# Two joined pairs of chunks instead of one in each feed-forward, with one plain chunk between them

## The chip, the cores and the metric

One Trainium2 chip; the kernel runs on one of its cores. The metric is the device time of one launch in microseconds, the median of three runs: 2022.09 us before (2021.98 to 2022.65). Five engines matter here, each with its own in-order queue: TensorE (PE, with its weight loads as PEld), VectorE (DVE), ScalarE (ACT) and SyncE (SP), whose queue starts the DMA transfers; GpSimd (POOL) has next to nothing to do.

## The reference

Two blocks are run one after the other on an input of 256 rows by 1024 columns in float32, each with two layers. A layer of the first block is a feed-forward, a hybrid mixer and a second feed-forward; a layer of the second block is a mixer, a cross attention and a feed-forward. That makes six feed-forwards: four in the first block (layer 0, layer 0, layer 1, layer 1) and two in the second. Both blocks have the same hidden width.

```python
def swiglu_ffn(h, w_gate, w_up, w_down):
    return (jax.nn.silu(h @ w_gate) * (h @ w_up)) @ w_down     # h: 256 x 1024, hidden width 2816

x = x + 0.5 * rms_norm(swiglu_ffn(rms_norm(x, g_pre), w_gate, w_up, w_down), g_post)
```

Only the feed-forwards are touched by the change.

## The kernel before

**Products in three passes.** Every float32 operand is split into a high part (rounded, made by ACT) and a low part (the rest, made by DVE as operand minus high part), and a product is high x high + high x low + low x high. So a weight tile of 128 x 2048 (1 MB, called a unit) costs one ACT instruction (`high`, L1421), one DVE instruction (`weight_low`, L2113) and 24 matmuls of 128x128 by 128x512: 4 blocks of rows by 3 passes by 2 halves of the 256 rows.

**Chunks.** The hidden width of 2816 is worked off in 11 chunks (0 to 10) of 256 columns. A plain chunk c has two units for gate and up, `("gu", c, 0)` and `("gu", c, 1)`, and one for the down projection, `("down", c)`. Between them ACT makes the silu (L1517), DVE the hidden product (`hidden`, L2198), then DVE takes it apart into 16-bit planes (`part`, L2209), SP's queue transposes the planes by DMA (`turn_halves`, L567 and L571), DVE puts them together again (`join`, L2223), and ACT (`hidden_high`, L1533) and DVE (`hidden_low`, L2204) split the result. The down unit of a chunk waits for that last step (`gT_ready`). It stands after gate and up of the next chunk.

**A joined pair.** For the chunk numbers in `PAIRS`, chunk c and chunk c+1 are made together. Gate of both chunks is one 1024 x 512 matrix and up another; with the 256 rows of the input cut in two, the 2 x 2 by 2 x 2 product of blocks is made with seven block products instead of eight, by Strassen's scheme in Winograd's form. A block product is half a unit: 12 matmuls (L876), and it has one `high` and one `weight_low` of its own. TensorE's order in a pair is 1, 5, 2, 6, then the down unit of chunk c-1, then 3, 7, 4. What the seven products need beside their operands:

- sums of the input's blocks, once per feed-forward: `rows_whole` (one DVE instruction of 128x2048, L2235), `row_sums` (four of 128x512, L2239 to L2242), their high part on ACT (`sum_hi`, L1563) and their low part on DVE (`row_sums_low`, two of 128x1024, L2246 and L2248);
- sums of the weights' blocks, four DVE instructions of 128x2048 for each pair: T1 (L2260), T2 (L2265), T4 (L2272), T3 (L2276). T1 needs the weights of products 1 and 7, T2 those of product 3 too, T4 those of product 2. Products 5, 6, 7 and 4 use T1, T2, T3 and T4;
- sums of the results: four DVE additions (L2280), one more (L2314), and the hidden products of the pair (L2309, and L2320 twice).

**Order and buffers.** The order of all engines is written out by hand. DVE's order in a pair (the function `pair` of the DVE part) is T2, T4, low 2, low 6, join(c-1), low of down c-1, hidden_low(c-1), T3, low 3 and so on; T1, low 1, low 5 and `hidden` and `part` of chunk c-1 stand in front of it, in the chunk before the pair. That chunk is made by `chunk`, or by `chunk_behind` where it comes right after another pair; a `chunk_behind` has the two joins of the pair in it. TensorE waits in a pair for `hid_ready` (hidden of chunk c-1) before product 1, for `low_ready` before each product and for `gT_ready` before the down unit. The raw weights have a ring of five slots, loaded by SP in the order of `ffn` and `pair` there, each when the unit that held its slot is done (`FREED_BY`); the high parts have a ring of four.

In the program before, `PAIRS = (5,)`: chunks 5 and 6 are a pair, all others are plain. The row sums are spread over chunks 2, 3 and 4. In the first feed-forward the ACT queue also starts the loads of constants and gains after chunk 2, and DVE makes the tables for rotary angles after chunk `HOOK`; in the third, ACT starts the load of the memory input ahead of chunk 2 (`memory_load`); in the fourth, DVE splits the turned memory (L2709) ahead of the first `hidden_low`.

Of the kernel before, what the change touches and what calls it, by code (L numbers as in the profile page):

```python
# [31 lines left out]
ACT = mybir.ActivationFunctionType  # L32
# [25 lines left out]
NEG = -1e30  # L58


PAIRS = (5,)
JOIN_ON_ACT = False
HOOK = 7


def _ffn_order():
# [139 lines left out]
def _program(ctx, nc, d, out, counted):  # L206
# [7 lines left out]
    done, after = S.done, S.after  # L214
# [301 lines left out]
    def _(sp):  # L516
# [45 lines left out]
        def turn_halves(L, n, c):  # L562

            sp.wait_ge(halves_ready, L.turns(n, c))
            if c in SECOND:
                for t in range(TT):
                    sp.dma_start_transpose(second_halves_T[:, t, :, :],  # L567
                                           second_halves[:, t, :, :].rearrange("p b n -> p (b n)")).then_inc(second_turned, 16)
                return
            for t in range(TT):  # L570
                sp.dma_start_transpose(halves_T[:, t, :, :], halves[:, t, :, :].rearrange("p b n -> p (b n)")).then_inc(  # L571
                    halves_turned, 16)

        def ffn(L, n, k0, wg, wu, wd, ffn_ahead=None):
            for kh in range(2):
                gate_up(L, k0 + kh, kh, wg, wu, 0)
            if ffn_ahead:
                turn_halves(*ffn_ahead, NCHUNK - 1)

            def chunk(c):  # L580
                if c - 3 in PAIRS:
                    turn_halves(L, n, c - 3)
                gate_up(L, k0 + AT["gu", c, 0], 0, wg, wu, c)
                if c - 3 in PAIRS:
                    turn_halves(L, n, c - 2)
                if c > 2 and c - 2 not in PAIRS and c - 3 not in PAIRS:
                    turn_halves(L, n, c - 2)
                gate_up(L, k0 + AT["gu", c, 1], 1, wg, wu, c)
                if c == 2:
                    turn_halves(L, n, 0)  # L590
                if c - 2 in PAIRS:
                    down(L, k0 + AT["down", c - 2], wd, c - 2)
                if c < NCHUNK - 2:
                    down(L, k0 + AT["down", c - 1], wd, c - 1)

            def pair(c):
                if c - 3 in PAIRS:
                    turn_halves(L, n, c - 3)
                    turn_halves(L, n, c - 2)
                square(L, k0 + AT["p", c, 1], wg, 0, c * FC)  # L600
                if c - 3 not in PAIRS:
                    turn_halves(L, n, c - 2)
                square(L, k0 + AT["p", c, 7], wu, 0, c * FC)
                square(L, k0 + AT["p", c, 3], wu, 512, c * FC)
                square(L, k0 + AT["p", c, 2], wg, 512, c * FC)
                turn_halves(L, n, c - 1)
                down(L, k0 + AT["down", c - 1], wd, c - 1)

            for c in range(1, NCHUNK - 1):
                if c in PAIRS:  # L610
                    pair(c)
                elif c not in SECOND:
                    chunk(c)
            end, c = k0 + U_FFN - 1, NCHUNK - 1
            for kh in range(2):
                gate_up(L, end - 4 + kh, kh, wg, wu, c)
            turn_halves(L, n, c - 2)
            for i in range(3):
                down(L, end - 2 + i, wd, c - 2 + i)
            turn_halves(L, n, c - 1)  # L620
# [789 lines left out]
    def _(act):  # L1410
# [100 lines left out]
        def ffn(L, n, j, k0):  # L1511
            f = L.ffn(n)
# [106 lines left out]
                hidden(0)  # L1619
            silu(L, k0 + 3, 1)  # L1620
            high(L, k0 + 4 + AHEAD)
            for c in range(2, NCHUNK - 1):
                if c in SECOND:
                    continue
                if c in PAIRS:
                    pair(k0 + AT["p", c, 1], c)
                    continue
                if memory_here(L, n) and c == 2:
                    memory_load()
                (chunk_behind if c - 2 in PAIRS else chunk)(k0 + AT["gu", c, 0], c)  # L1630
                if L.sub0 + j == 0 and c == 2:
                    gain(post_g, 0, 1, post_loaded)
                    at, width = CONST["inv_freq"]
                    for at, end in ((P, at), (at + width, CONST_ARRAY.shape[1])):
                        act.dma_start(const[:, at:end], d["const"][:, at:end]).then_inc(const_loaded, 16)
                if L.sub0 + j == 0 and c == 8:
                    rope()
                if memory_here(L, n) and c == (9 if NCHUNK - 3 in SECOND or NCHUNK - 4 in SECOND else 8):
                    memory_std(L.l)
# [454 lines left out]
    def _(dve):  # L2094
# [97 lines left out]
        def ffn(L, n, j, k0):  # L2192
# [41 lines left out]
            def rows_whole():  # L2234
                then(V.tensor_tensor(sums, flat(hT_hi[:, :, :]), flat(hT_lo[:, :, :]), ALU.add), "whole")  # L2235
# [136 lines left out]
            else:  # L2372
                weight_low(L, k0 + 2 + AHEAD)
                join(0)
                hidden_low(0)
            weight_low(L, k0 + 3 + AHEAD)
            hidden(1)
            part(1)
            weight_low(L, k0 + 4 + AHEAD)
            for c in range(2, NCHUNK - 1):  # L2380
                if c in SECOND:
# [794 lines left out]
```

## Time and profile before

| | us |
|---|---|
| median of three runs (lowest, highest) | 2022.09 (2021.98, 2022.65) |
| the profiled execution, whole time | 2023.4 |
| the profiled execution, span of the trace | 2021.6 |
| PE busy in the span | 2000.0 (99%) |
| DVE busy | 1589.3 (79%) |
| ACT busy | 1169.2 (58%) |
| granted TensorE clock, mean | 0.999 of full speed |

The six feed-forwards lie at about 12 to 191, 431 to 611, 611 to 791, 1029 to 1212, 1432 to 1612 and 1835 to 2015 us. The profile gives for each engine when it was busy and, for idle time, which engine or transfer ended it. A matmul of 512 columns is shown with some 0.39 us, but the matmuls overlap: their starts are 0.227 us apart, and counts and durations of a run of them tell the rate. The large DVE instructions are shown with 2.28 us and start 2.20 us apart.

### The profile page before, as it was taken

What the parts mean: (1) busy time and instruction counts of PE and PEld (TensorE: products, weight loads), DVE (VectorE), ACT (ScalarE), POOL (GpSimd) and SP (SyncE); (2) the same over time, 40 slices, a digit from 0 to 9 for tenths busy, and PEclk for the clock granted to TensorE, in tenths of its full rate; (3) what the DMA queues carried; (4) which work ended last, traced back from release to release, by engine and by line L of the source; (5) the groups of instructions that cost most, each with busy time, mean ns of one, the idle gap of its engine ahead of it and who ended that gap; (6) DMA issues with size and microseconds to landing.
All of it is one profiled execution on the core that took longest, in us unless ns stands there. A gap on an engine that the chain in (4) does not pass through costs nothing.

```text
span 2021.6 us, 24239 instructions
## 1 busy us (share of the span) xinstructions
PE 2000.0 (99%) x9442; PEld 1639.1 (81%) x9442; DVE 1589.3 (79%) x2024; ACT 1169.2 (58%) x1438; POOL 0.2 (0%) x4
## 2 busy tenths in 40 slices
PE   8999999999999999999999999999999999999998
PEld 6788887888888888887888888888888887888887
DVE  6896899778867877899768967966788679667885
ACT  6455657664546555666564646756645466566453
POOL 0000000000000000000000000000000000000000
PEclk9999999999999999999999999999999999999999
DMA  8766764567777675764557767554667674546764
GB/s 261 235 204 183 225 201 146 171 194 208 221 211 240 202 229 171 225 189 146 186 184 208 223 184 212 189 157 148 191 214 215 190 226 161 176 141 186 223 211 121
DMA packets 339122, 394.54 MB, mean 195 GB/s; under 512 B 123824, under 2 KB 235072, under 8 KB 339008
## 3 DMA queue, kind: packets, MB, share of 16 engines
q1 hardware_dynamic: 334912, 381.94, 61.8%
q10 hardware_dynamic: 4096, 11.05, 1.5%
q8 instruction: 75, 1.23, 0.3%
q14 instruction: 39, 0.32, 0.1%
HBM read 365.66 MB, written 1.05 MB: 181 GB/s over the span
## 4 chain that ended last, share of the span: by engine, by line
PE 88%; DVE 6%; DMA 2%; ACT 2%; issue 1%; SPq 1%; ACTq 0%; DVEq 0%
PE ps L739 75%; PE ps L876 5%; DVE w_lo L2113 2%; PE ps L810 1%; DVE scratch L2530 1%; DMA raw<-in_ffn_w_up 1%; PE ps L1361 1%; PE ps L1342 1%; DVE x L2163 0%; ACT w_hi L1421 0%; DMA raw<-in_w_co 0%; DVE scratch L2567 0%; PE ps L925 0%; PE ps L833 0%; DMA x<-in_x 0%
## 5 line engine op out<-in xcount | busy, mean ns | idle before, releaser
L2113 DVE TENSOR_TENSOR w_lo<-raw,w_hi 128x2048 fp32r<-128x2048 f32 x336 | 766.3, 2286 | 135.2 <-ACT w_hi L1421 133.2
L1421 ACT ACTIVATE w_hi<-raw 128x2048 fp32r<-128x2048 f32 (+2 forms) x340 | 643.6, 1897 | 378.5 <-PE ps L739 169.9
L739 PE MATMUL ps<-w_hi,hT_hi 128*128 128x512 f32 x1856 | 731.5, 394 | 0.0
L739 PE MATMUL ps<-w_lo,hT_hi 128*128 128x512 f32 x1856 | 723.5, 390 | 0.0
L739 PE MATMUL ps<-w_hi,hT_lo 128*128 128x512 f32 x1856 | 699.4, 389 | 0.0
L739 PEld LDWEIGHTS ps<-w_hi,hT_hi 128*128 128x128 f32 x1856 | 348.9, 188 | 75.8 <-issue 5.5
L739 PEld LDWEIGHTS ps<-w_hi,hT_lo 128*128 128x128 f32 x1856 | 348.4, 188 | 73.4
L739 PEld LDWEIGHTS ps<-w_lo,hT_hi 128*128 128x128 f32 x1856 | 349.1, 188 | 69.6
L739 PE MATMUL ps<-w_hi,bT_hi 128*128 128x512 f32 x608 | 239.8, 394 | 0.6 <-DVE bT_lo L2204 0.5
L739 PE MATMUL ps<-w_hi,bT_lo 128*128 128x512 f32 x608 | 236.9, 390 | 0.0
L739 PE MATMUL ps<-w_lo,bT_hi 128*128 128x512 f32 x608 | 236.8, 390 | 0.0
L739 PEld LDWEIGHTS ps<-w_hi,bT_hi 128*128 128x128 f32 x608 | 114.1, 188 | 29.6 <-issue 5.7
L739 PEld LDWEIGHTS ps<-w_hi,bT_lo 128*128 128x128 f32 x608 | 114.2, 188 | 24.2
L739 PEld LDWEIGHTS ps<-w_lo,bT_hi 128*128 128x128 f32 x608 | 114.2, 188 | 22.7
L2223 DVE COPY scratch<-scratch 128x512 uint16<-128x512 uint16 x132 | 52.7, 454 | 63.8 <-DMA scratch<-scratch 63.8
L2530 DVE SCALAR_TENSOR_TENSOR scratch<-scratch,pack 128x256 f32<-128x256 f32 x240 | 98.2, 476 | 0.1
L1517 ACT ACTIVATE scratch<-ps,stat 128x256 f32<-128x256 f32 x108 | 45.2, 470 | 88.1 <-PE ps L739 87.1
L1660 ACT ACTIVATE scratch<-ps,stat 128x512 f32<-128x512 f32 (+1 forms) x84 | 51.3, 663 | 73.8 <-PE ps L739 73.6
L2198 DVE SCALAR_TENSOR_TENSOR scratch<-ps,stat,scratch 128x256 f32<-128x256 f32 x108 | 47.1, 477 | 47.4 <-ACT scratch L1517 47.2
L1467 ACT ACTIVATE hT_hi<-ps,gains_T 128x128 fp32r<-128x128 f32 x192 | 53.7, 380 | 37.7 <-PE ps L810 36.5
L1533 ACT ACTIVATE bT_hi<-scratch 128x512 fp32r<-128x512 f32 x48 | 30.2, 629 | 72.3 <-DVE scratch L2223 72.2
L2136 DVE SCALAR_TENSOR_TENSOR hT_lo<-ps,gains_T,hT_hi 128x128 fp32r<-128x128 f32 x192 | 52.8, 342 | 11.9 <-ACT hT_hi L1467 11.9
(340 smaller groups left out, 1742.4 us busy)
## 6 DMA issues: line engine op xcount, KB each, us to landing
raw<-in_w_in SPq DMA_DIRECT2D x160, 512.0 KB, 4.6
raw<-in_ffn_w_down SPq DMA_DIRECT2D x88, 512.0 KB, 4.4
raw<-in_ffn_w_gate SPq DMA_DIRECT2D x86, 512.0 KB, 4.1
raw<-in_ffn_w_up SPq DMA_DIRECT2D x86, 512.0 KB, 5.0
raw<-in_w_gate SPq DMA_DIRECT2D x44, 512.0 KB, 4.0
raw<-in_w_up SPq DMA_DIRECT2D x44, 512.0 KB, 5.0
raw<-in_w_down SPq DMA_DIRECT2D x44, 512.0 KB, 4.5
raw<-in_w_out SPq DMA_DIRECT2D x32, 512.0 KB, 4.2
```

The costliest lines, as they stand in the source:

```text
L739: mm = nc.tensor.matmul(bank(t, half), act[:, tiles[i], t * P:(t + 1) * P], w, start=start and (i, n) == steps[0], stop=stop and (i, n) == ...
L876: mm = nc.tensor.matmul(ps[:, bank, :], act, w[:, i, :], start=start and (i, m) == (0, 0), stop=(i, m) == (3, 2), skip_group_check=True)
L1421: nc.scalar.activation(dst, src, ACT.Copy).then_inc(high_ready, 1)
L1467: nc.scalar.activation(hT_hi[:, 4 * kh + c, t * P:(t + 1) * P], ps[:, 6 - 2 * t + kh, c * P:(c + 1) * P], ACT.Copy, scale=pre_gain(L, j, 4 ...
L1517: silu_t = nc.scalar.activation(sil[:, t, :], ps[:, bank + t, 0:FC], ACT.Silu, scale=rstd_in[:, t:t + 1])
L1533: nc.scalar.activation(dst, joined, ACT.Copy).then_inc(gT_hi_ready, 1)
L1660: last = nc.scalar.activation(dst[:, t, :], src[:, t, :], func, scale=scale[:, t:t + 1])
L2113: V.tensor_tensor(lo, src, flat(hi), ALU.subtract).then_inc(low_ready, 1)
L2136: turned_low = V.scalar_tensor_tensor(hT_lo[:, c, t * P:(t + 1) * P], ps[:, 6 - 2 * t + kh, (c % 4) * P:(c % 4 + 1) * P], pre_gain(L, j, c ...
L2198: up = V.scalar_tensor_tensor(hid[:, t, :], ps[:, bank + t, FC:2 * FC], rstd_in[:, t:t + 1], sil[:, t, :], ALU.mult, ALU.mult)
L2223: both = V.tensor_copy(dst[:, t, :, :, :], src[:, t, :, :, :])
L2530: V.scalar_tensor_tensor(conv_y[:, c, :], src, w[:, c, i:i + 1], conv_y[:, c, :], ALU.mult, ALU.add).then_inc(*done("conv_taps", f"tap{i}_ ...
```

## The change

`PAIRS` becomes (3, 6): chunks 3 and 4 are one pair, chunks 6 and 7 another, and chunk 5 is a plain chunk between them, made by `chunk_behind` with its `ahead` branches, since a pair follows it. The row sums are no longer spread over chunks 2 to 4: `rows_whole` moves ahead of `hidden(1)` and `row_sums` behind `part(1)` on DVE, and the high part of the sums follows `high` of down 1 on ACT. On SP the turn of a first pair's second chunk (`turn_halves(L, n, c - 2)`) comes after the load of product 1's weights of the second pair instead of before it. The tables of the first feed-forward move from chunk 7 to chunk 8 on DVE and from 8 to 9 on ACT; the statistics of the memory input follow chunk 9 instead of chunk 8.

```diff
-PAIRS = (5,)
+PAIRS = (3, 6)
 JOIN_ON_ACT = False
-HOOK = 7
+HOOK = 8
@@ SP, pair(c)
                 if c - 3 in PAIRS:
                     turn_halves(L, n, c - 3)
-                    turn_halves(L, n, c - 2)
                 square(L, k0 + AT["p", c, 1], wg, 0, c * FC)
-                if c - 3 not in PAIRS:
-                    turn_halves(L, n, c - 2)
+                turn_halves(L, n, c - 2)
                 square(L, k0 + AT["p", c, 7], wu, 0, c * FC)
@@ ACT, ffn
             high(L, k0 + 4 + AHEAD)
+            if PAIRS[0] == 3:
+                act.wait_ge(*after("forms", "rows", f))
+                nc.scalar.activation(sum_hi[:, :, :], sums, ACT.Copy).then_inc(*done("held", "rows_high", f))
             for c in range(2, NCHUNK - 1):
...
-                if L.sub0 + j == 0 and c == 8:
+                if L.sub0 + j == 0 and c == 9:
                     rope()
@@ DVE, ffn
             weight_low(L, k0 + 3 + AHEAD)
+            if PAIRS[0] == 3:
+                rows_whole()
             hidden(1)
             part(1)
+            if PAIRS[0] == 3:
+                row_sums()
             weight_low(L, k0 + 4 + AHEAD)
```

The whole program has 72 matmuls fewer (12 for each feed-forward) and 66 DVE instructions more. Two places of DVE's order follow. The line numbers of the changed kernel are higher by one in DVE's part up to `rows_whole` and by five at its end: L2199 of it is L2198 before, L2261 is L2260.

First, DVE in the first feed-forward from the low part of the unit `("gu", 2, 1)` on (it is the second of the x2), before the change:

```order
L2113 TENSOR_TENSOR w_lo<-raw,w_hi 128x2048 x2
L2198 SCALAR_TENSOR_TENSOR scratch<-ps,stat,scratch 128x256 x2
L2209 COPY scratch<-scratch 128x1024
L2113 TENSOR_TENSOR w_lo<-raw,w_hi 128x2048
L2223 COPY scratch<-scratch 128x2x2x128 x2
L2113 TENSOR_TENSOR w_lo<-raw,w_hi 128x2048
L2204 TENSOR_TENSOR bT_lo<-scratch,bT_hi 128x512
```

and with the change, behind that same x2 row:

```order
L2236 TENSOR_TENSOR scratch<-hT_hi,hT_lo 128x2048
L2199 SCALAR_TENSOR_TENSOR scratch<-ps,stat,scratch 128x256 x2
L2210 COPY scratch<-scratch 128x1024
L2240 TENSOR_TENSOR scratch<-scratch 128x4x128
L2241 TENSOR_TENSOR scratch<-scratch 128x4x128
L2242 TENSOR_TENSOR scratch<-scratch 128x4x128
L2243 TENSOR_TENSOR scratch<-scratch 128x4x128
L2114 TENSOR_TENSOR w_lo<-raw,w_hi 128x2048
L2247 TENSOR_TENSOR sp<-scratch,sum_hi 128x1024
L2249 TENSOR_TENSOR sum_lo<-scratch,sum_hi 128x1024
L2224 COPY scratch<-scratch 128x2x2x128 x2
L2205 TENSOR_TENSOR bT_lo<-scratch,bT_hi 128x512
```

The row right behind is T1 of the first pair. The whole preparation of the row sums now stands between the low parts of chunk 2's weights and T1, and `rows_whole` stands ahead of `hidden(1)`.

Second, DVE between the last low part of the first pair and the next chunk, before the change (chunk 7, `chunk_behind` without a pair ahead of it):

```order
L2223 COPY scratch<-scratch 128x2x2x128 x2
L2204 TENSOR_TENSOR bT_lo<-scratch,bT_hi 128x512
L2113 TENSOR_TENSOR w_lo<-raw,w_hi 128x2048
L2223 COPY scratch<-scratch 128x2x2x128 x2
L2204 TENSOR_TENSOR form_lo<-scratch,form_lo 128x512
L2113 TENSOR_TENSOR w_lo<-raw,w_hi 128x2048
L2198 SCALAR_TENSOR_TENSOR scratch<-ps,stat,scratch 128x256 x2
L2209 COPY scratch<-scratch 128x1024
L2113 TENSOR_TENSOR w_lo<-raw,w_hi 128x2048 x2
```

and with the change (chunk 5, with the second pair ahead), from its second join on:

```order
L2224 COPY scratch<-scratch 128x2x2x128 x2
L2205 TENSOR_TENSOR form_lo<-scratch,form_lo 128x512
L2261 TENSOR_TENSOR scratch<-raw 128x2048
L2114 TENSOR_TENSOR w_lo<-raw,w_hi 128x2048
L2199 SCALAR_TENSOR_TENSOR scratch<-ps,stat,scratch 128x256 x2
L2210 COPY scratch<-scratch 128x1024
L2114 TENSOR_TENSOR form_lo<-scratch,w_hi 128x2048
L2266 TENSOR_TENSOR scratch<-raw,scratch 128x2048
L2273 TENSOR_TENSOR scratch<-raw,scratch 128x2048
L2114 TENSOR_TENSOR w_lo<-raw,w_hi 128x2048
```

The two joins of the first pair are followed at once by T1, T2 and T4 of the second (L2261, L2266, L2273), where before plain low parts stood.

## Rows read from the trace of the kernel before

**Rows 1.** The page's first part: busy us of each engine.

```profile
PE 2000.0 (99%) x9442; PEld 1639.1 (81%) x9442; DVE 1589.3 (79%) x2024; ACT 1169.2 (58%) x1438; POOL 0.2 (0%) x4
```

**Rows 2.** Waits of PE: total us, times, longest.

```profile
PE ps L876 <- DVE w_lo L2113: 2.1, 2, 1.8
```

**Rows 3.** Windows, fifth feed-forward: us, busy (records), then clock, DMA share, GB/s.

```profile
1439.00:1611.00 172.00, 172.00 (x757) 141.59 (x756) 135.13 (x129) 91.74 (x91) 0.00 (x0) 1.00 0.68 207
```

**Rows 4.** Chain of waits, fifth feed-forward: start us, us, what.

```profile
1511.52 11.03 PE ps L876 x48
1522.56 5.68 PE ps L739 x24
1528.24 8.33 PE ps L876 x36
1536.56 73.62 PE ps L739 x324
```

**Rows 5.** Timeline of DVE, fifth feed-forward, chunk 1: start us, us, line, operation.

```profile
1458.85 0.87 DVE L2198 SCALAR_TENSOR_TENSOR scratch<-ps,stat,scratch 128x256 f32<-128x256 f32 x2
1459.76 0.69 DVE L2209 COPY scratch<-scratch 128x1024 uint16<-128x1024 uint16 x1
1460.37 2.28 DVE L2113 TENSOR_TENSOR w_lo<-raw,w_hi 128x2048 fp32r<-128x2048 f32 x1
```

**Rows 6.** The same, chunks 3 and 4: row sums, join, hidden_low, T1.

```profile
1483.74 0.68 DVE L2239 TENSOR_TENSOR scratch<-scratch 128x512 f32<-128x512 f32 x1
...
1486.63 2.29 DVE L2113 TENSOR_TENSOR w_lo<-raw,w_hi 128x2048 fp32r<-128x2048 f32 x1
...
1494.69 1.22 DVE L2246 TENSOR_TENSOR sp<-scratch,sum_hi 128x1024 fp32r<-128x1024 f32 x1
...
1496.96 0.79 DVE L2223 COPY scratch<-scratch 128x512 uint16<-128x512 uint16 x2
1498.45 0.69 DVE L2204 TENSOR_TENSOR bT_lo<-scratch,bT_hi 128x512 fp32r<-128x512 f32 x1 [0.70 <-ACT bT_hi L1533]
1501.38 2.29 DVE L2260 TENSOR_TENSOR scratch<-raw 128x2048 f32<-128x2048 f32 x1 [2.24 <-DMA raw<-in_w_up]
```

**Rows 7.** The same, in the pair and behind it: T2, lows 2 and 6, hidden_low(4), hidden_low(6).

```profile
1509.51 2.28 DVE L2265 TENSOR_TENSOR scratch<-raw,scratch 128x2048 f32<-128x2048 f32 x1
...
1514.11 2.28 DVE L2113 TENSOR_TENSOR w_lo<-raw,w_hi 128x2048 fp32r<-128x2048 f32 x1
1516.31 2.28 DVE L2113 TENSOR_TENSOR form_lo<-scratch,w_hi 128x2048 fp32r<-128x2048 f32 x1
...
1521.70 0.69 DVE L2204 TENSOR_TENSOR bT_lo<-scratch,bT_hi 128x512 fp32r<-128x512 f32 x1
...
1550.53 0.69 DVE L2204 TENSOR_TENSOR form_lo<-scratch,form_lo 128x512 fp32r<-128x512 f32 x1 [0.70 <-ACT form_lo L1533]
```

**Rows 8.** Timeline of ACT: high part of down 4, which waited for its load.

```profile
1517.55 1.91 ACT L1421 ACTIVATE w_hi<-raw 128x2048 fp32r<-128x2048 f32 x1
```

**Rows 9.** Timeline of SP's queue: load of down 4; first load behind both turns.

```profile
1512.16 1.05 SPq L531 DMA_DIRECT2D raw<-in_w_down  x2
...
1545.58 0.58 SPq L531 DMA_DIRECT2D raw<-in_w_gate  x1
```

**Rows 10.** Chain of waits, first feed-forward (and the fourth, last row).

```profile
35.14 16.62 PE ps L739 x72
...
52.20 10.47 DMA raw<-in_ffn_w_up
...
1055.50 49.25 PE ps L739 x216
```

**Rows 11.** Timeline of DVE: hidden(1), first and fourth feed-forward; join(1), third.

```profile
39.32 0.87 DVE L2198 SCALAR_TENSOR_TENSOR scratch<-ps,stat,scratch 128x256 f32<-128x256 f32 x2
...
646.01 0.80 DVE L2223 COPY scratch<-scratch 128x512 uint16<-128x512 uint16 x2 [4.70 <-DMA scratch<-scratch]
...
1059.68 0.86 DVE L2198 SCALAR_TENSOR_TENSOR scratch<-ps,stat,scratch 128x256 f32<-128x256 f32 x2
```

## The prediction

> **What bounds the kernel now.** I read the page's first part, then the waits of PE, the windows of one feed-forward, the chain of waits, and the timelines of DVE, ACT and SP in that feed-forward. TensorE is busy for 2000.0 of 2021.6 us [rows 1]; its waits for DVE's low parts sum to 2.1 us in the whole run, one of 1.8 among them [rows 2]. In the fifth feed-forward PE is busy for all 172 us of its window and DVE for 135.1, which leaves DVE 37 us [rows 3]. The chain there is PE alone: 324 matmuls in 73.62 us, 0.2272 each, so a unit of 24 takes 5.45 us; the seven block products take 11.03 + 8.33 = 19.36 us for 84 matmuls, 0.2305 each or 2.76 a block [rows 4].
>
> **What is removed.** Six feed-forwards lose 12 matmuls each. A plain pair of chunks has 96 x 0.2272 = 21.81 us of gate and up, a joined one 19.36, so 2.45 us go for each feed-forward and 14.7 in all, if PE never waits.
>
> **What is added, in DVE's time.** A large DVE instruction starts 2.20 after the one before it (1514.11 to 1516.31) [rows 7]. A second pair has four of them for T1 to T4 (8.8), three more low parts (7 against 4, 6.6), and small sums that come to some 3 us net: about 18.5 us for each feed-forward. DVE's 37 idle us hold that on the whole. What counts is where it stands, and the first pair starts three units after chunk 2 begins. I follow DVE's order in the fifth feed-forward, on the clock of the trace before; nothing differs until 1458.85, when the low part of ("gu", 2, 1) is through.
>
> **The first pair.** rows_whole 2.20, to 1461.05. hidden(1) 0.91 and part(1) 0.61 [rows 5], to 1462.57; PE wants hidden(1) at 1462.5 and has it at 1462.1, so nothing waits. The four row sums take 2.89 (1483.74 to 1486.63), to 1465.46; low of down 1 2.20; the two low halves of the sums 2.27 (1494.69 to 1496.96); join(1), its wait for ACT and hidden_low(1) 1.49 + 0.61 [rows 6]: 1472.03. Before, DVE then sat idle 2.24 for a load before T1 [rows 6]; here the load of product 7's weights (issued behind the turn, near 1465.2) is in by then. T1 and lows 1 and 5, 6.60: 1478.63. Only now comes hidden(2), ready at 1479.50, and 0.17 later PE can start (hidden_low(4) ended at 1522.39, its down unit started at 1522.56 [rows 7, 4]). Product 1 is due six units before 1511.52, at 1478.8 [rows 4], and starts at 1479.7: **wait 0.9**. part(2) ends at 1480.15; T2, T4 and low 2 follow, low 2 from 1484.55 to 1486.83. Products 1 and 5 are through at 1485.2, product 2 starts at 1487.0: **wait 1.8**. Before, T2 started 2.0 us ahead of product 1 (1509.51 against 1511.52); here it starts 0.45 behind it.
> Products 2 and 6 end at 1492.5. Down 2 needs its low part and hidden_low(2). Its load is issued 2.65 us after part ends (1512.16 against T2's start 1509.51) and its high part starts 5.39 later [rows 9, 8]: 1488.2, ready at 1490.1. Low and hidden_low end at 1493.0, PE starts at 1493.15: **wait 0.65**. The same step waited 0.17 before. From here to the end of the pair every distance is that of before, 29.4 us earlier.
>
> **Chunk 5 and the second pair.** This is the place that the trace before does not show. hidden_low(4), formerly of chunk 6 at 1550.53 [rows 7], starts at 1521.1, and T1 at 1521.75. The load that it needs comes right behind the second turn, as the load of 1545.58 did [rows 9]: 1516.2 + 5.4 = 1521.6, just in time. T1, low 1: 1526.15; hidden(5), part(5): 1527.65; low 5, T2, T4: 1534.25; low 2 ready at 1536.53. PE leaves the first pair at 1536.56 - 29.4 and has four units (21.8): product 1 is due at 1528.95, products 1 and 5 are through at 1534.5, product 2 starts at 1536.7: **wait 2.2**. Low 6, join(5), low of down 5 and hidden_low(5) end at 1542.35, and down 5 starts at 1542.5: **wait 0.3**. From the first pair to here DVE is never idle but for some 0.7 us each time ACT makes a high part for it. Down 5 starts 19.9 us after its counterpart of before (1522.56), with three units fewer behind it (16.4): the feed-forward ends **3.6 us later**. The terms say the same: waits of 5.85 against a saving of 2.45. Behind the second pair DVE has plain chunks, in which it gets ahead again as before.
>
> **Six feed-forwards.** 6 x 3.6 = 21.5. Beside that:
> - In the fourth, hidden(1) starts at 1059.68 [rows 11], since the memory's split stands before it, and down 0 at 1055.50 [rows 10]. With rows_whole ahead, hidden(1) is ready at 1062.8, down 0 is through at 1061.0: 2.0 more, and product 1 waits 1.2 instead of 0.9. I take 2.3, less the 0.3 that is left of [rows 2] after the 1.8: +2.0.
> - In the first, the same: hidden(1) at 39.32 [rows 11], down 0 at 35.14 [rows 10], 2.3 more. ACT's load of constants and gains made one weight load take 10.47 us [rows 10] instead of 5.4. It now starts behind the high part of product 2, so it meets the turn of chunk 2 and the load of down 2, which PE waits for already. Bounds 0 and 5.1; I take 3.5, near the upper, as nothing covers it. The wait of 1.8 before [rows 2] is there too and goes: +4.0.
> - In the third, the load of the memory held join(1) back by 4.70 us of idle time [rows 11]. It now starts behind sum_hi, when the load for T1 is half through, and T1 has 0.8 us of slack. Bounds 0 and 4.7; as only the rest of that load is hit, I take a third: +1.6.
> - Moved tables (the first) and memory statistics (the third) stand behind the pairs, where DVE and ACT have gaps of 1 to 3 us in each chunk: 0. Without that cover, they would cost their length, some 5 us in each place.
>
> The sum is 21.5 + 2.0 + 4.0 + 1.6 = 29.1. The profiled execution took 2023.4 us as a whole (span 2021.6), so 2052.5; the runs have a median 1.3 below it: **2051 us**.
>
> A page rule on the size of DVE's step: the Trainium skill, "VectorE: DVE Perf Modes", The TRN2 errata, gives 2.29 us for a float32 tensor_tensor of 2048 elements, and under The DRAIN you can't avoid lets the next start only when the pipe is empty. The duration agrees (2.28 in rows 7), the step does not: it is 2.20. With 2.29 the large instructions on the way would add about 1 us to each feed-forward and the sum would be some 2057; the measured step decides.
>
> **Rivals.**
> - *DVE's idle time covers it.* For: 37 idle us in 172 [rows 3] against 18.5 added. Then PE never waits and the time is 2022.1 - 14.7 = **2007**. It needs T2 of the first pair to start by 1477.8 (product 2's due time 1484.3, less 0.17, less 2.20 twice and 2.28) where the order gives 1480.15, and T2 of the second to start 2.2 us sooner. The break-even point is a sum of waits of 2.45 us in each feed-forward, so it decides itself there. Against: DVE works through in a fixed order, and its idle time before the first pair was that 2.24 and the waits for turns in chunks 0 to 2, which the row sums use up. The Trainium skill, "Perfetto Trace Analysis", Identifying the Most-Contended Engine, says to improve the engine with the highest occupancy first, which is PE here: by that rule alone the change gives this rival's time. Rows 1 agree that PE is the one; that another engine takes over for a stretch is what they can't show.
> - *Only the second pair waits.* If DVE enters the first pair as early as it did before (turns land sooner, ACT doesn't hold it up), 3.35 go, and the extras of the first and fourth shrink to about 3: 6 x (2.5 - 2.45) + 3 to 8 gives **2026 to 2032**.
> - *Loads are late, too.* The ring has five slots, and behind the first pair three loads and two turns are issued within 8 us. If T1 of the second pair gets its weights 2 us later than I take (the slow load of rows 10 was 5 later), the waits grow by as much: 29.1 + 12 gives **2063**.
> - *The change does not do what it says:* the order shows 72 matmuls fewer and 66 DVE instructions more, so I leave this out.
>
> **How the numbers follow.** My forecast 0.68; the second pair alone waits 0.10; late loads 0.11; DVE covers it 0.09; a time within 0.2% of before (4 us, about what a measurement of this kernel can tell from no change) 0.02. The forecast's own bounds: 1 us either way in each feed-forward (6), and the two unknown loads at 0 (-5.1) or at their upper ends (+4.7): 2040 to 2062. The range goes on to the second and third rivals: 2030 to 2065. Faster 0.09, same 0.03, slower 0.88.
>
> **What would show it.** In each feed-forward of the changed profile: a wait of the block products (L874 there) for a low part of about 2 us in each pair, and one of under 1 for hidden_low before the down unit; product 1 of the first pair waiting for hidden(2); DVE without gaps from part(1) to the end of the second pair; PE's busy time about 16 us less, its waits 35 to 45 in all. The fourth and first feed-forward should have a wait of ("gu", 2, 0) for hidden(1). The forecast is wrong if DVE has idle time right before T2 of either pair, or if PE's long waits are for loads.

## The result, and the profile after

The changed kernel takes 2062.80 us (median of four runs, 2060.86 to 2066.83) against 2022.05 beside it: ratio 1.0203 (95% interval 1.0186 to 1.0221), 40.8 us slower. The forecast was slower by 29; the time lies inside the range, at its upper edge. The profiled execution has a span of 2059.0 us (2021.6 before) and a mean granted clock of 0.992 (0.999 before).

The page's first part, and PE's waits in the feed-forwards (engine, line, releaser: total us, times, longest), which answer to [rows 1, 2]:

```profile
PE 2002.9 (97%) x9370; PEld 1633.7 (79%) x9370; DVE 1697.5 (82%) x2090; ACT 1208.0 (59%) x1456; POOL 0.2 (0%) x4
```

```profile
PE ps L874 <- DVE w_lo L2114: 27.1, 11, 3.2
PE ps L874 <- DVE scratch L2199: 7.8, 6, 3.4
...
PE ps L737 <- DVE scratch L2199: 2.1, 2, 1.3
...
PE ps L737 <- DVE bT_lo L2205: 1.1, 2, 0.8
```

The waits sum to 38.1 us in 21 starts (2.6 us in three before), where 35 to 45 were forecast, and none is for a load (but for the input at the very start, as before). But PE's busy time was to fall by about 16 us and rose by 2.9, with 72 matmuls fewer. So the matmuls that are left take longer somewhere. The chain of waits of the fifth feed-forward shows where; it answers to [rows 4] (start us, us, what), on a clock that is 25.93 us later:

```profile
1513.23 5.75 PE ps L874 x24
1519.02 5.74 PE ps L737 x24
1524.76 8.33 PE ps L874 x36
1533.08 5.45 PE ps L737 x24
...
1563.36 8.61 PE ps L874 x24
1571.97 5.49 PE ps L737 x24
1577.45 8.33 PE ps L874 x36
```

Block products 2 and 6 are 24 matmuls. In the first pair they take 5.75 us, in the second 8.61. PE's timeline at that place (last column: idle time ahead of the instruction and what ended it):

```profile
1560.12 0.40 PE L874 MATMUL ps<-w_hi,sum_lo 128*128 128x512 f32 x1
1563.36 0.77 PE L874 MATMUL ps<-w_hi,hT_hi 128*128 128x512 f32 x1 [2.85 <-DVE w_lo L2114]
1563.92 0.63 PE L874 MATMUL ps<-w_lo,hT_hi 128*128 128x512 f32 x1
1564.35 0.63 PE L874 MATMUL ps<-w_hi,hT_lo 128*128 128x512 f32 x1
```

After the wait of 2.85 us the starts are 0.43 us apart instead of 0.23. The windows (columns of [rows 3]) give the clock:

```profile
1555.00:1560.00 5.00, 5.00 (x23) 4.08 (x23) 4.87 (x3) 2.93 (x2) 0.00 (x0) 1.00 0.60 159
1560.00:1565.00 5.00, 2.15 (x7) 1.46 (x6) 5.00 (x3) 3.42 (x4) 0.00 (x0) 0.77 0.88 313
1565.00:1570.00 5.00, 5.00 (x14) 3.85 (x14) 5.00 (x6) 2.43 (x2) 0.00 (x0) 0.55 0.02 3
1570.00:1575.00 5.00, 5.00 (x23) 4.09 (x22) 5.00 (x4) 3.87 (x3) 0.00 (x0) 1.00 0.69 210
```

The granted clock fell from its level of 2.4 GHz to that of 1.2 GHz at the end of the wait and came back some 7 us later (the window from 1562.7 to 1569.5 has 0.50). 14 matmuls fit into the window that holds 23 otherwise. Products 2 and 6 of the second pair take 7.11, 7.17, 5.80, 7.34, 8.61 and 7.34 us in the six feed-forwards, where 5.8 is what they take at full clock behind a wait.

The clock fell in the first pair too, in two feed-forwards: in the first, behind a wait of 1.81 us ahead of product 2 (products 2 and 6 took 7.36 us), and in the third, behind a wait of 3.45 us ahead of product 1 (all four took 13.90 us against 11.03 in [rows 4]). The window of the first:

```profile
66.80:74.20 7.40, 7.36 (x24) 5.55 (x24) 5.03 (x5) 4.20 (x3) 0.00 (x0) 0.77 0.91 299
```

DVE in the two pairs of the fifth feed-forward, which answers to [rows 6, 7]: T1, hidden(2), T2, T4 and low 2 of the first pair; then hidden_low(4), T1, T2, T4 and low 2 of the second pair, and the first sum of its results, ahead of which DVE is idle for 2.05 us:

```profile
1498.08 2.28 DVE L2261 TENSOR_TENSOR scratch<-raw 128x2048 f32<-128x2048 f32 x1
...
1504.69 0.87 DVE L2199 SCALAR_TENSOR_TENSOR scratch<-ps,stat,scratch 128x256 f32<-128x256 f32 x2
...
1506.20 2.28 DVE L2266 TENSOR_TENSOR scratch<-raw,scratch 128x2048 f32<-128x2048 f32 x1
1508.59 2.29 DVE L2273 TENSOR_TENSOR scratch<-raw,scratch 128x2048 f32<-128x2048 f32 x1
1510.80 2.29 DVE L2114 TENSOR_TENSOR w_lo<-raw,w_hi 128x2048 fp32r<-128x2048 f32 x1
...
1547.04 0.69 DVE L2205 TENSOR_TENSOR form_lo<-scratch,form_lo 128x512 fp32r<-128x512 f32 x1 [0.70 <-ACT form_lo L1531]
1548.18 2.29 DVE L2261 TENSOR_TENSOR scratch<-raw 128x2048 f32<-128x2048 f32 x1 [0.45 <-DMA raw<-in_w_up]
...
1556.31 2.28 DVE L2266 TENSOR_TENSOR scratch<-raw,scratch 128x2048 f32<-128x2048 f32 x1
1558.72 2.29 DVE L2273 TENSOR_TENSOR scratch<-raw,scratch 128x2048 f32<-128x2048 f32 x1
1560.93 2.28 DVE L2114 TENSOR_TENSOR w_lo<-raw,w_hi 128x2048 fp32r<-128x2048 f32 x1
...
1580.35 0.69 DVE L2281 TENSOR_TENSOR scratch<-scratch,ps 128x512 f32<-128x512 f32 x1 [2.05 <-PE ps L874]
```

Less the 25.93, T2 of the first pair starts at 1480.27 (forecast 1480.15), hidden(2) at 1478.76 (1478.63), T1 of the second pair at 1522.25 (1521.75).

From start to end, by the chain of waits of both kernels, the six feed-forwards are 6.6, 5.2, 7.7, 5.8, 7.0 and 6.2 us longer, together 38.5; what lies between them is 1.1 shorter. The rows account for it: 35.5 more of waits, less the 14.7 saved, plus 12.9 for the seven falls of the clock (8.7 in second pairs, 1.6 and 2.6 in the two first pairs), plus 4.9 for 18 more starts behind a wait (24 matmuls take 5.78 us in the chain instead of 5.51, so some 0.27 each). That makes 38.6.

### The profile page after: what moved, and what is told of

It is laid out like the page before. It is cut to its first block, busy times and chain, and to the rows that moved or that the text cites. A ratio compares the mean times of both kernels' runs of the same rounds, so it can differ in the third digit from the quotient of the medians.

```text
span 2059.0 us, 24293 instructions
## 1 busy us (share of the span) xinstructions
PE 2002.9 (97%) x9370; PEld 1633.7 (79%) x9370; DVE 1697.5 (82%) x2090; ACT 1208.0 (59%) x1456; POOL 0.2 (0%) x4
## 4 chain that ended last, share of the span: by engine, by line
PE 70%; DVE 18%; DMA 4%; ACT 4%; issue 2%; SPq 2%; DVEq 0%; ACTq 0%
PE ps L737 55%; PE ps L874 8%; DVE w_lo L2114 5%; DMA raw<-in_ffn_w_up 2%; DVE scratch L2261 1%; DVE form_lo L2114 1%; PE ps L808 1%; DVE scratch L2535 1%; DVE scratch L2273 1%; ACT w_hi L1419 1%; DVE scratch L2266 1%; DVE scratch L2199 1%; SPq L567 1%; PE ps L1359 1%; PE ps L1340 1%
## 5 line engine op out<-in xcount | busy, mean ns | idle before, releaser
L737 PE MATMUL ps<-w_lo,hT_hi 128*128 128x512 f32 x1664 | 648.4, 390 | 0.0
L737 PE MATMUL ps<-w_hi,hT_lo 128*128 128x512 f32 x1664 | 624.8, 390 | 0.0
L737 PEld LDWEIGHTS ps<-w_hi,hT_hi 128*128 128x128 f32 x1664 | 312.6, 188 | 71.3 <-issue 5.5
L737 PEld LDWEIGHTS ps<-w_hi,hT_lo 128*128 128x128 f32 x1664 | 312.4, 188 | 65.9
L737 PEld LDWEIGHTS ps<-w_lo,hT_hi 128*128 128x128 f32 x1664 | 312.8, 188 | 61.9
L737 PE MATMUL ps<-w_hi,bT_hi 128*128 128x512 f32 x560 | 221.1, 395 | 1.2 <-DVE bT_lo L2205 1.1
L737 PE MATMUL ps<-w_lo,bT_hi 128*128 128x512 f32 x560 | 218.2, 390 | 0.0
L1419 ACT ACTIVATE w_hi<-scratch 128x2048 fp32r<-128x2048 f32 x36 | 69.0, 1916 | 52.3 <-DVE scratch L2261 27.1
L2114 DVE TENSOR_TENSOR form_lo<-scratch,w_hi 128x2048 fp32r<-128x2048 f32 x36 | 82.2, 2283 | 0.0
L874 PE MATMUL ps<-w_hi,sum_hi 128*128 128x512 f32 x192 | 76.2, 397 | 0.0
L1465 ACT ACTIVATE hT_hi<-ps,gains_T 128x128 fp32r<-128x128 f32 x192 | 53.7, 379 | 38.1 <-PE ps L808 36.9
```

Source lines behind the costliest of these rows:

```text
L737: mm = nc.tensor.matmul(bank(t, half), act[:, tiles[i], t * P:(t + 1) * P], w, start=start and (i, n) == steps[0], stop=stop and (i, n) == ...
L874: mm = nc.tensor.matmul(ps[:, bank, :], act, w[:, i, :], start=start and (i, m) == (0, 0), stop=(i, m) == (3, 2), skip_group_check=True)
L1419: nc.scalar.activation(dst, src, ACT.Copy).then_inc(high_ready, 1)
L1465: nc.scalar.activation(hT_hi[:, 4 * kh + c, t * P:(t + 1) * P], ps[:, 6 - 2 * t + kh, c * P:(c + 1) * P], ACT.Copy, scale=pre_gain(L, j, 4 ...
L2114: V.tensor_tensor(lo, src, flat(hi), ALU.subtract).then_inc(low_ready, 1)
```

## The experiments

Medians in us; "before" was run beside each group (2022.58, 2022.86 and 2022.66). The last column is what block products 2 and 6 of the second pair take in the six feed-forwards of the profiled execution (about 5.8 behind a wait with no fall of the clock). In e15 and e16 product 4 of the second pair is computed from other numbers, with the same instructions.

| kernel | median (lowest, highest) | ratio to before (95%) | products 2 and 6, second pair |
|---|---|---|---|
| changed | 2062.80 (2060.86, 2066.83) | 1.0203 (1.0186, 1.0221) | 7.11 7.17 5.80 7.34 8.61 7.34 |
| e4, first pair alone | 2049.52 (2048.14, 2050.10) | 1.0132 (1.0117, 1.0147) | no second pair |
| e5, second pair alone | 2020.67 (2019.41, 2021.91) | 0.9989 (0.9980, 0.9999) | waits of 0.3 at most |
| e8, rows_whole early | 2053.45 (2051.35, 2055.61) | 1.0152 (1.0137, 1.0168) | 5.80 7.36 7.36 7.35 7.35 5.79 |
| e1, both waits filled | 2058.91 (2057.53, 2059.49) | 1.0178 (1.0161, 1.0195) | 5.78 5.80 5.78 5.75 5.78 5.80 |
| e14, second wait filled | 2056.56 (2055.86, 2059.38) | 1.0170 (1.0156, 1.0184) | 5.76 5.80 5.76 5.63 5.78 5.78 |
| e15, T4 out of the way | 2056.65 (2055.64, 2057.63) | 1.0167 (1.0153, 1.0181) | wait split |
| e16, e15 and e8 | 2043.80 (2043.27, 2046.27) | 1.0106 (1.0092, 1.0120) | wait split |
| e7, turns ahead of the load | 2077.48 (2075.34, 2080.88) | 1.0273 (1.0258, 1.0289) | 7.12 7.35 7.36 8.22 8.09 8.27 |
| e2, joins on ACT | 2070.58 (2064.89, 2073.89) | 1.0243 (1.0226, 1.0260) | 5.76 7.11 7.10 7.36 7.35 7.17 |
| e9, e2 and e8 | 2060.81 (2054.41, 2063.14) | 1.0184 (1.0166, 1.0203) | 7.35 8.45 7.37 8.46 7.34 7.22 |
| e3, before with e2's joins | 2025.02 (2022.39, 2025.97) | 1.0009 (1.0000, 1.0019) | |

My theory after the result: the waits come from DVE's order as forecast, and a further term is the lower clock behind the long wait of the second pair. The rivals were that the slower matmuls have another cause, that loads or the second pair by itself make the waits, and that any relief of DVE would show in full.

### Each pair by itself (e4, e5)

```diff
-PAIRS = (3, 6)
+PAIRS = (3,)     # e4
+PAIRS = (6,)     # e5
```

> PAIRS = (3,): the first pair of the change alone, with its row sums close before it; chunks 6 and 7 plain. Saves nothing against before (both have one pair). Theory (each pair has its own wait, and only the second one brings the clock down): waits of 0.9 + 1.7 + 0.7 for each feed-forward and no fall of the clock outside the third feed-forward, so 6 x 3.4 = 20, and 5 to 8 for the first, third and fourth: 2045 to 2050. Rival (the loss of the change is in the second pair): the first pair waits less without the second, 2025 to 2035.

> PAIRS = (6,): the second pair of the change alone, with the row sums spread over chunks 3 to 5 as before. Theory (the second pair waits because DVE comes out of the first with work left, and product 2 of it is due only 4 units behind): no wait of over 0.5 us in the pair and no fall of the clock; the time of before, 2020 to 2025. Rival (a pair at chunk 6 waits by itself for its loads or forms, whatever stands ahead of it): 2.9 us of wait and 2 to 3 us of the lower clock for each feed-forward, 2045 to 2055.

Both theories came true: e4 lies inside its 2045 to 2050, e5 inside its 2020 to 2025. PE's waits of e4, then of e5:

```profile
PE ps L874 <- DVE w_lo L2114: 9.0, 5, 1.8
PE ps L874 <- DVE scratch L2199: 7.9, 6, 3.6
...
PE ps L737 <- DVE scratch L2199: 3.4, 2, 1.7
PE ps L737 <- DVE bT_lo L2205: 2.9, 3, 2.2
```

```profile
PE ps L737 <- DVE bT_lo L2205: 1.6, 3, 0.7
...
PE ps L874 <- DVE w_lo L2114: 0.4, 2, 0.3
```

The first pair alone costs 26.9 us against the one pair of before. My terms for it were 6 x (0.9 + 1.8 + 0.65) = 20.1 and 7.6 of extras, 27.7. They were all waits, and e4's waits are only 20.6 longer than before (23.2 against 2.6); the rest goes to starts behind a wait and to one fall of the clock, in the third feed-forward. A pair at chunk 6 with its row sums spread costs nothing (1.9 us less than before, within what counts here as no change). Behind the first pair the same pair adds 2062.80 - 2022.05 - 26.9 = 13.9, where the forecast had 6 x (2.5 - 2.45) = 0.3. So most of the error is in the second pair, and it is not the pair's own. The rows give nearly the same: 18.0 of waits, 8.7 of clock and 1.6 of starts, less 14.7, is 13.6.

### Filling the wait (e1, e14)

```diff
                 block(c, 5, summed, 4, 1, 5, True)
+                for i in range(FILL[0] if c == PAIRS[0] else FILL[1]):    # e1: (6, 12); e14: (0, 12)
+                    nc.tensor.matmul(ps[:, 7, :], hT_hi[:, i % 4, 0:P], sum_hi[:, 0:2, :], start=True, stop=True,
+                                     skip_group_check=True)
```

> The changed kernel, with matmuls added whose result nobody reads (6 in the first pair, 12 in the second, each about 0.23 us, in an unused bank), between block products 5 and 2, where TensorE otherwise stands still for 1.7 and 2.9 us. Theory (the granted clock falls to its lower level because TensorE stood still for 2.9 us): the clock stays at 1.00 behind product 2 of the second pair, its matmuls start 0.23 us apart instead of 0.43, the pair of block products 2 and 6 takes 5.5 us instead of 7.1 to 8.6, and the waits themselves are about as long as before or filled; 10 to 14 us less than the changed kernel: 2049 to 2053. Rival (the slower matmuls come from something else that goes on at that moment, DVE's or a transfer's traffic, not from TensorE's standing still): the matmuls behind stay at 0.43 us and the time stays at 2063 or rises by what the added matmuls cost (up to 18 x 0.23 = 4 us in each feed-forward where the wait doesn't cover them).

> The changed kernel with the 12 unread matmuls between block products 5 and 2 of the second pair alone, none in the first. The profile with both groups of them gave 5.78 us for block products 2 and 6 of every second pair, where the changed kernel has 5.80 to 8.61, 8.7 us less in sum, but a median of only 3.9 us less; two waits of down 2 in the first pair were 1 us longer there. Theory (those two and the rest are the run-to-run scatter of transfers or the price of the 6 in the first pair, the lower clock costs what the rows say): 8.7 us less than 2062.8, so 2052 to 2056. Rival (the lower clock is worth less than the rows say, because what follows would have waited for DVE anyway): 2058 to 2060 again, with the time found in waits of down 5 or of product 3.

PE's timeline of e1 at the second pair of the fifth feed-forward, and its windows there:

```profile
1561.13 2.94 PE L885 MATMUL ps<-sum_hi,hT_hi 128*128 128x512 f32 x12
1564.34 0.47 PE L875 MATMUL ps<-w_hi,hT_hi 128*128 128x512 f32 x1 [0.27 <-DVE w_lo L2118]
1564.65 0.39 PE L875 MATMUL ps<-w_lo,hT_hi 128*128 128x512 f32 x1
```

```profile
1560.00:1565.00 5.00, 4.73 (x21) 3.61 (x20) 5.00 (x3) 4.41 (x4) 0.00 (x0) 1.00 1.01 372
1565.00:1570.00 5.00, 5.00 (x23) 3.83 (x22) 5.00 (x6) 2.44 (x2) 0.00 (x0) 1.00 0.29 74
```

DVE and the transfers do the same as in the changed kernel, low 2 comes as late, and the clock stays at 1.00: the rival of another cause is out. In all six feed-forwards products 2 and 6 take 5.8 us or less in both kernels; the sum is 34.7 in e1 and 34.5 in e14 against 43.4, so the rows say 8.7 to 8.9. The medians give 3.9 and 6.2, below what I expected both times: e1 stands above its 2049 to 2053 and below its rival's 2063, e14 between its two ranges.

Two things account for most of the rest. From product 1 of the first pair to product 3 of the second, e14's profiled execution is 8.2 us shorter than the changed kernel's, close to what the rows say, but it is 3.3 us longer outside of these stretches (4.9 shorter as a whole): 0.8 before the first, 0.8 between the third and the fourth feed-forward, 1.6 between the fifth and the sixth. In e1 it is 3.0 us longer there, and the largest piece, 1.5, lies elsewhere, between the fourth and the fifth. No edit touches these places; that this is scatter from run to run was not shown. And e1 has a fall of its own: in the first feed-forward down 2 waits 1.80 us there for `hidden_low`, and the 24 matmuls behind take 7.33. The wait for down 2 (0.81 in the changed kernel, 2.38 in e14) is a case where the clock costs nothing. Its load is late: DVE stands idle 2.37 us ahead of the unit's low part, in e14 as in the changed kernel, and down 2 starts 15.8 us behind product 1 in both. In the changed kernel the matmuls ahead of it ran at the lower clock and filled 1.6 us of that wait.

The Trainium skill, "TensorE: Matmul & The Clock Gate", What's actually happening, says that the lower level is the default state and that activity lifts it; these rows agree, since matmuls that compute nothing of use hold the clock up.

### Moving one DVE instruction out of a wait's way (e8, e15, e16)

```diff
@@ e8: DVE, start of a feed-forward (and taken out ahead of hidden(1))
+            if PAIRS[0] == 3:
+                rows_whole()
             hidden(0, 0)
@@ e15: DVE, pair(c), for c = 6 only
                 t2(c)
-                t4(c)
                 low_form(c, 2)
...
                 low_form(c, 3)
+                dve.wait_ge(*after("forms", f"t3_{c}", f))
+                b12 = landed(c, 7)
+                V.tensor_tensor(form[2], b12, b12, ALU.add).then_inc(*done("forms", f"t4_{c}", f))
```

> The changed kernel with rows_whole (one DVE instruction of 2.20 us) ahead of hidden(0), where DVE stands idle for 2.1 us, instead of ahead of hidden(1). Theory (DVE's backlog of work in a fixed order makes the waits of the first pair): hidden(2), T2 and low 2 of the first pair come 2.2 us earlier; the wait of product 1 for hidden(2) (0.8 to 1.0) goes and that of product 2 falls from 1.7 to about 0.6, together 2.0 to 2.2 us for each feed-forward, in the first and fourth too (hidden(1) wait gone); the second pair is as before, wait and clock too: 12 to 14 us less, 2049 to 2051. Rival (the first pair waits for its transfers or for ACT's high parts): DVE is idle for as long somewhere ahead of T2 instead, and the time falls by less than 4 us: 2059 to 2063.

> The changed kernel with the instruction for T4 of the second pair (2.20 us of DVE) moved from ahead of low 2 to behind low 3, where DVE stands idle for 2.05 us; since low 2 overwrites an operand of T4, it adds another tile to itself instead, so product 4 of the second pair is computed from other numbers. Theory (TensorE waits in the second pair for DVE's chain T1 to low 2, and the clock falls because of that wait): product 2 waits 0.7 to 0.8 us instead of 2.9 to 3.2, down 5 not at all, block products 2 and 6 take 5.8 us or less in all six: 6 x 2.2 + 8.7 = 22 less: 2039 to 2043. Rival 1 (the clock term is noise): 13 less, 2049 to 2051. Rival 2 (the wait only moves on to down 5 or product 3): 2055 to 2063.

> The same, and rows_whole ahead of hidden(0) (which alone gave 2053.5 against 2062.8). Product 4 of the second pair is again computed from other numbers. Theory: the waits left are those of the first pair (1.0 to 1.8 for each feed-forward as in that run) and 0.75 in the second, together about 2.45, which is what the twelve fewer matmuls save; with 4 to 8 for falls of the clock and the loads of the first and third feed-forward the time is 2026 to 2034. Rival 1 (only the matmuls count once the second wait is short): at or below the time of before, 2014 to 2022. Rival 2 (the two gains overlap): 2038 to 2045.

e8 fell by 9.3 us, most of the 12 to 14. DVE's idle time before hidden(0) took the instruction in:

```profile
1469.74 2.29 DVE L2236 TENSOR_TENSOR scratch<-hT_hi,hT_lo 128x2048 f32<-128x2048 f32 x1
1472.07 0.88 DVE L2199 SCALAR_TENSOR_TENSOR scratch<-ps,stat,scratch 128x256 f32<-128x256 f32 x2
```

The wait for hidden(2) is gone in four feed-forwards and product 2 of the first pair waits 0.6 instead of 1.8 in three. In the fifth feed-forward, down 2 waits 1.14 in return, which in the changed kernel the longer wait ahead of it covered. PE's waits in the second pair of e15 (fifth feed-forward) show the same thing more clearly:

```profile
1561.98 0.50 PE L875 MATMUL ps<-w_hi,hT_hi 128*128 128x512 f32 x1 [0.65 <-ACT scratch L1585]
1568.07 0.47 PE L738 MATMUL ps<-w_hi,bT_hi 128*128 128x512 f32 x1 [0.26 <-DVE bT_lo L2206]
...
1577.47 0.48 PE L875 MATMUL ps<-w_hi,sum_hi 128*128 128x512 f32 x1 [0.90 <-DVE w_lo L2115]
```

With T4 gone from there, product 2 waits 0.5 to 1.5 us instead of 2.9 to 3.2, now for ACT, which has to copy product 1's result away. But product 7 waits 0.9 for its low part, because the moved instruction stands ahead of it, and down 5 up to 0.3. Of the 13 us of waits that were to go, 1.0 went: all waits in e15's feed-forwards sum to 37.1 us against 38.1, the rest moved on, as rival 2 had it. What did go are the falls of the clock in the second pairs: e15's mean granted clock is 0.998, and two falls are left, in first pairs. It gains 6.2 us, as much as e14, but it has more starts behind a wait to pay for (38 against 21), so its gain is not a clean price of the clock. e16 adds e8's gain, and a little more: 2043.80, above my 2026 to 2034 and inside rival 2 (2038 to 2045). Its waits in the feed-forwards sum to 27.4 us (12.6 for low parts of block products, 5.8 and 2.7 for low parts of the down and gate-and-up units, 2.0 for hidden products, 4.3 for ACT), and less the 14.7 saved that is 12.7 of the 21.1 us that it is still slower than before. Its 34 starts behind a wait, at some 0.27 each, are 9.2 more; less the 3.4 that waits and starts cost before, this gives 18.5 of the 20.0 us between the two profiled executions. The clock did not fall in its feed-forwards. What is left after that I did not follow up.

### Loads and ACT (e7, e2, e9, e3)

```diff
@@ e7: SP, pair(c), as before the change
                 if c - 3 in PAIRS:
                     turn_halves(L, n, c - 3)
+                    turn_halves(L, n, c - 2)
                 square(L, k0 + AT["p", c, 1], wg, 0, c * FC)
-                turn_halves(L, n, c - 2)
+                if c - 3 not in PAIRS:
+                    turn_halves(L, n, c - 2)
@@ e2, e9 (with e8's edit) and e3 (on the kernel before)
-JOIN_ON_ACT = False
+JOIN_ON_ACT = True
```

> The changed kernel with one part of the change undone: SP issues both turns of the first pair ahead of the load of product 1's weights of the second pair, as the code stood. Theory (the second pair's T1 and low 1 stand right behind their loads): the load of product 1 is issued 2.5 us later, low 1 and all behind it on DVE come about 1 us later, the wait of product 2 in the second pair grows from 2.9 to about 3.9, with at least as much time at the lower clock: 2066 to 2075. Rival (the second pair waits for DVE's backlog alone, loads have slack): the turn of chunk 4 and so hidden_low(4) come sooner or nothing changes: 2060 to 2064.

> The changed kernel with JOIN_ON_ACT = True: the two copies of each join (0.80 us of DVE, and 0.7 us in which DVE waits for ACT's high part right behind) are made by ACT in front of its hidden_high. Theory (DVE's fixed order is what TensorE waits for): DVE saves one join ahead of product 1 of the first pair and one ahead of hidden_low(2), and two ahead of T1 of the second, but T1 of the second is also held by the load of product 7's weights, so little is gained there: 0.5 to 1.5 us for each feed-forward, 2054 to 2060. Rival (any relief of DVE shows in full): 2 joins of 1.5 us each ahead of the second pair as well, its wait falls from 2.9 to below 1 and the clock stays up: 2040 to 2046.

> The changed kernel with both: rows_whole ahead of hidden(0) (which alone gave 2053.5) and the joins on ACT. Theory: the first pair's wait of product 2 falls from 1.8 to about 0.2, of product 1 to 0, that of down 2 stays near 0.8; the second pair keeps its wait of 2.9 to 3.1 and its fall of the clock, since T1 of it is held by the load: 2046 to 2051. Rival (any relief of DVE shows in full): the second pair's wait goes too: 2030 to 2038, still above before, or below it if no wait of over 1 us is left (2020).

> Control: the kernel before with JOIN_ON_ACT = True. Theory (before, DVE has slack everywhere that a join lies): no change, 2020 to 2024. Rival (ACT's order suffers from the joins, its waits for turns hold back high parts): 2026 or more, and then the two runs with the joins on ACT have to be read with that cost in them.

e7 is 14.7 us slower than the changed kernel, 2.5 above what I gave it at most. DVE and PE in its fourth feed-forward:

```profile
1151.10 2.29 DVE L2263 TENSOR_TENSOR scratch<-raw 128x2048 f32<-128x2048 f32 x1 [2.04 <-DMA raw<-in_ffn_w_up]
```

```profile
1166.28 0.77 PE L876 MATMUL ps<-w_hi,hT_hi 128*128 128x512 f32 x1 [3.83 <-DVE w_lo L2116]
```

T1 of the second pair now waits 2.04 us for product 7's weights (0.54 there in the changed kernel), PE waits 3.83 us, and the clock falls behind that wait in all six feed-forwards. So T1 stands between two limits: DVE's work out of the first pair, and a load that SP can issue only behind a turn. The reordering on SP was worth its place.

The joins on ACT were a miss: 7.8 us slower, where both theories had a gain. DVE and ACT of e2 in chunk 5 of the fifth feed-forward:

```profile
1553.26 0.69 DVE L2205 TENSOR_TENSOR form_lo<-scratch,form_lo 128x512 fp32r<-128x512 f32 x1 [2.72 <-ACT form_lo L1531]
1554.34 2.29 DVE L2261 TENSOR_TENSOR scratch<-raw 128x2048 f32<-128x2048 f32 x1 [0.39 <-DMA raw<-in_w_up]
```

```profile
1551.15 1.41 ACT L1526 ACTIVATE scratch<-scratch 128x512 uint16<-128x512 uint16 x2 [3.54 <-DMA scratch<-scratch]
```

ACT itself waits 3.54 us for the turn and needs 1.41 us for the two copies (DVE 0.79), and DVE, freed of them, waits 2.72 us for the result and then 0.39 for the same load as ever. DVE gains nothing before T1. Product 2 of the second pair waits longer than in the changed kernel in three feed-forwards (3.75 to 3.82). In the first pair of this feed-forward the clock fell too, behind a wait of 1.82 us: products 2 and 6 took 7.37 us, against 5.75 behind 1.78 in the changed kernel. e9 was expected at 2046 to 2051 and loses the same against e8 (7.4 us); in the first feed-forward of its profiled execution down 2 alone waits 6.46 us, behind a late load, and its runs lie up to 8.7 us apart, so this figure is rough. e3, expected at no more than 2024, is 2.2 us above the kernel before (ratio 1.0009, interval from 1.0000), hardly more than no change, so most of the loss comes with the two pairs.

## Why the prediction was right in its course and short in its size

- **The saving.** The rates held: 8.33 us for 36 matmuls of block products, and each block pair without a wait 5.5. 72 matmuls went, 14.7 us.
- **First pair.** Forecast waits 0.9, 1.8, 0.65; in the fifth feed-forward 0.81, 1.78, and some 0.3 (the down unit took 5.74 instead of 5.45). This is the mechanism of the prediction, a preparation moved into one chunk in DVE's fixed order, and e8 bears it out. The last wait was too large: of the twelve for `hidden_low` (0.65 and 0.3), the trace lists two, 0.81 in the first feed-forward and 0.27 in the sixth. That the whole term came out at 26.9 (e4) against 27.7 is in part luck, since e4's waits are 20.6 of it.
- **Second pair, its wait.** Forecast 2.2, measured 2.96, 2.98, 3.10, 2.95, 2.85 and 3.17, in sum 18.0 against 13.2. In the fifth, T1 came 0.50 later than forecast, 0.45 of it a wait for the load that I had called just in time, and there is another gap of 0.2 ahead of T4. The late load of my third rival is there, in this size (0.45 to 0.76); I had priced it at 2 us. That the measured time equals this rival's 2063 is chance.
- **Second pair, the clock: the step that failed.** The prediction counted PE's waits and took every matmul behind them at 0.23 us ("The terms say the same: waits of 5.85 against a saving of 2.45"). Neither the clock's level nor the price of a start behind a wait was among its terms. In five of six feed-forwards the clock fell at product 2's wait, at 1.3 to 2.8 us each: 8.7 us by the rows, 6.2 by the medians (e14). With 4.8 for the longer waits, these two shares are 11 to 14, and e4 leaves 13.6 above the forecast for the second pair. Over all six feed-forwards and both pairs the clock is 12.9 us by the rows and the starts 4.9, together 17.8. The total is only 11.7 us above the forecast, mostly because the forecast's waits were too long in sum: 42.7 with the extras below, against 35.5 more than before. So it is partly luck that the time lies inside the range: two errors work against each other.
- **First, third, fourth feed-forward.** Forecast 7.6, 5.2 and 5.6 in all, measured 6.6, 7.7 and 5.8. The extras stood for something, but not each as I sized it. Hidden(1) was late by 1.26 us in the first and 0.83 in the fourth, where I took 2.3. In the third, T1's load took 8.76 us in the chain (5.51 to 5.69 at the second pairs) and made hidden(2) late, a wait of 3.45 us, and the clock fell there. The memory's load was issued at the same moment (656.24 and 655.99), which fits my reason, but no run takes it away. The moved tables and statistics cost nothing, as forecast: the last 252 matmuls take 57.30 us in the first, third and fifth feed-forward alike.
- **Rivals.** "DVE's idle time covers it" is refuted; the sum of DVE's busy time rose by 108 us and the profile still leaves DVE 361 idle us, in other places. The Trainium skill's rule ("Perfetto Trace Analysis", Identifying the Most-Contended Engine), taken on the whole kernel, pointed at PE's instructions; this case shows that removing 72 of them loses 40.8 us when their cost goes to an engine that is late at that place. "Only the second pair waits" is refuted by e4. Two of the rivals' sums were off without effect: T2 of the first pair would have had to start by 1477.45, not 1477.8, and the terms given for the second rival add up to some 2025 to 2030, not 2026 to 2032.

No version with two pairs that I ran is as fast as the kernel before. The fastest kernel of the study is e5, one pair at chunk 6, 0.9989 (0.9980 to 0.9999) of the time before. What I did not try is a version in which DVE's sums for the second pair are made by another engine; each low part is written over its own operand, so T4 can't simply wait until after low 2.

## What to carry to other kernels

An engine's idle share says nothing about a chain that stands in one place: follow its order there, instruction by instruction, to the point where the bound engine needs it. When that gives TensorE a wait like the ones here (1.8 to 3.2 us), price the start behind it (some 0.27 us here) and price the matmuls behind it at the lower clock as well, as a term with a chance, and look at PE's busy time against its count of matmuls: more time for fewer of them is the sign. And when a wait is taken away, look for the next one a few us behind it, which it had covered.

## What the runs showed of the hardware that was not expected

- The granted clock falls at waits that are short against a feed-forward, and not each time at the same wait. Over all kept traces with the first pair at chunk 3: at product 2's waits of 2.66 to 3.84 us in the second pair it fell in 26 of 30 (five of six in the changed kernel), at those of 1.78 to 1.82 us in the first pair in 6 of 37 (e.g. 7.37 us for products 2 and 6 in e2's fifth feed-forward and e15's second). At the waits of 0.2 to 1.6 us in e15's second pairs it stayed at 1.00 in all six feed-forwards.
- One fall costs 24 matmuls 1.3 to 2.8 us. Twelve unread matmuls, 2.94 us by the record, kept it away in 12 cases of 12 (e1, e14).
- ACT takes 1.41 us for two copies of 128x512 16-bit elements (e2) for which DVE takes 0.79 (changed kernel).
